# Token-major residual stream in a transformer kernel, with the first two weight blocks behind each norm taken per token tile

## The chip, the cores and the metric

The kernel runs on one NeuronCore of a Trainium2 chip, as one program with one launch. The metric is device time in microseconds of that core. TensorE (PE) multiplies, VectorE (DVE) and ScalarE (ACT) work elementwise, SyncE (SP) issues the weight DMAs, GpSimd (POOL) has next to nothing to do.

## The reference

256 tokens of width 1024 pass through six feed-forward blocks and four mixers (called ev, od, da and ga); a second sequence of 256 tokens, the context, passes through three of the feed-forwards and gives keys and values to the last two mixers. Each of the ten sublayers of x has a norm ahead and a norm on its output:

```python
def rms_norm(x, g, eps=1e-6):
    y = xf * lax.rsqrt(jnp.mean(xf * xf, axis=-1, keepdims=True) + eps)
    return (y * g.astype(jnp.float32)).astype(x.dtype)
...
def swiglu(h, w_gate, w_up, w_down):
    return (jax.nn.silu(h @ w_gate) * (h @ w_up)) @ w_down
```

A sublayer is h = h + rms_norm(f(rms_norm(h, g_pre) (+ shift)), g_post), with f a swiglu (1024 to 2816 to 1024) or a mixer that ends in a 1024x1024 output product. In the first four sublayers the gains are weights; in the last six of x and those of the context they and the shift come from a modulation product of a conditioning vector (the lane "a" below).

## The kernel before, in words

**Layout.** Both sequences lie with channels on partitions: H is [128, 8, 256], tile k holding channels 128k to 128k+127 of all 256 tokens. Every weight matrix is streamed from HBM in blocks of 1 MB (128x2048 fp32; `load_weights`, L202, into four RAW slots). Each block is split into two f32r halves: whi on ACT and wlo on DVE in two parts (`splits` and `other_half`, L210 and L235; three whi buffers, four wlo). An activation is kept as a high and a low f32r part as well, and a product is the sum of three: high*whi, low*whi, high*wlo (`three`, L267). A product on PE (L264) has a 128x128 piece of the weight block as its stationary operand and 256 tokens of one k as its moving one; a block of 8 k and two output tiles is 48 such products (`two_tiles`, L277).

**Down and output products.** A feed-forward of x has 22 blocks of gate and up and then, for each of four pairs of output tiles, three pieces of the down matrix over 22 k. Behind each output tile comes `put_out` (L345): ACT squares it, squares it times the gain, and copies it times the gain; DVE adds both squares to running sums and H*y to a third.

**Norm.** `norm` (L588) adds those sums over partitions on PE (L538), takes root and reciprocal (L525, L527), spreads them over the partitions by a product with ones (L553), and gets the sum of squares of the new residual out of the three sums. Then for k = 0 to 7 DVE scales y (L631), adds it to H (L637), weights it (L686), ACT makes the high part (L691, or L689 without a shift), DVE the low part (L700 or L698). `first_blocks` (L316) takes the two blocks behind the norm as the k come: two high products of each of two output tiles, then the low one, with the second block five k behind.

**Lanes.** One Python program writes the instructions of all engines, in one order. x is the main sequence; "c" (context) and "a" (modulation) are generators that are stepped in between. At a yield of kind "D" (before a block) and "d" (in the middle of one) `pace` (L1185) gives the others a turn; at a yield of kind "L" (a wait of so many us) `fill` (L1170) puts in context blocks and modulation blocks by a model clock. A norm of x has five such "L" yields. Attention waits for the context's keys with `want` (L1211).

The engines run their own instructions strictly in the order written, each waiting at semaphores.

## Time and profile before

| | |
|---|---|
| median of 3 runs | 2719.95 us (2719.37 to 2722.16) |
| the profiled execution, span | 2725.8 us |
| PE busy | 2528.6 us (93%), 20780 instructions |
| weight loads busy (overlap PE) | 2395.9 us (88%) |
| DVE busy | 1707.1 us (63%) |
| ACT busy | 1248.6 us (46%) |
| DMA | 480.14 MB, mean 176 GB/s |
| mean granted TensorE clock | 0.966 of full speed |

The page gives no time of the profiled execution beside its span; the span is what the prediction's sum is made against. Durations of single instructions overlap their neighbours': what an engine gives in a row is read from the starts, not from the durations.

### The profile page before, as it was taken

Reading aid. Unit: us, or ns where it says so; the run is one execution under the profiler, and the core shown is the slowest. Engines: PE = TensorE matmul, PEld = TensorE weight load, DVE = VectorE, ACT = ScalarE, POOL = GpSimd, SP = SyncE. Lnnn points to the kernel's source line nnn. Section 1 sums busy time; section 2 is a strip of 40 time slices with the busy share of each in tenths; the row PEclk is TensorE's granted clock in tenths of the full one; section 3 lists DMA queues with packets and bytes.
Section 4 is the critical chain, followed back from the end, with each engine's and each line's share of the span. In section 5 each row is a group of like instructions: output and inputs, shape, how many; then the busy total and the mean of one; then the engine's idle time right before and its main releaser. Section 6 shows DMA issues by size and latency. Waiting matters only on the chain.

```text
span 2725.8 us, 48854 instructions
## 1 busy us (share of the span) xinstructions
PE 2528.6 (93%) x20780; PEld 2395.9 (88%) x20780; DVE 1707.1 (63%) x2804; ACT 1248.6 (46%) x1697; POOL 1.2 (0%) x6
## 2 busy tenths in 40 slices
PE   6799997999999999999888998999999999887998
PEld 5689996888998999999887898999999999756997
DVE  6565574656766565566767576577655557646655
ACT  4443453444544444445445554455444345435443
POOL 0000000000000000000000000000000000000000
PEclk9899999999999999999898999999999999888999
DMA  6456656533555665544351344555545555363453
GB/s 218 181 200 242 241 203 229 189 109 124 186 202 216 236 226 196 211 147 154 132 174 52 120 171 154 185 175 173 179 170 179 180 177 183 114 215 137 170 178 116
DMA packets 71591, 480.14 MB, mean 176 GB/s; under 512 B 8784, under 2 KB 9296, under 8 KB 17744
## 3 DMA queue, kind: packets, MB, share of 16 engines
q1 hardware_dynamic: 66240, 468.74, 48.8%
q10 hardware_dynamic: 5136, 8.28, 1.0%
q8 instruction: 166, 2.72, 0.4%
q14 instruction: 49, 0.40, 0.0%
HBM read 471.48 MB, written 1.05 MB: 173 GB/s over the span
## 4 chain that ended last, share of the span: by engine, by line
PE 73%; DVE 13%; ACT 7%; DMA 4%; issue 3%; ACTq 0%; DVEq 0%
PE bank L264 64%; ACT whi L223 4%; DVE wlo L243 2%; DMA raw<-w_main 2%; DVE wlo L230 2%; PE bank L1115 2%; DMA raw<-w_down 1%; PE bank L997 1%; PE bank L935 1%; DVE ARX L686 1%; DVE HX L637 1%; DVE tmpx L631 1%; PE bank L985 1%; PE bank L553 0%; PE bank L1639 0%
## 5 line engine op out<-in xcount | busy, mean ns | idle before, releaser
L264 PE MATMUL bank<-HNX_hi,whi 128*128 128x256 f32 x2968 | 866.2, 293 | 64.3 <-DVE wlo L243 24.4
L223 ACT ACTIVATE whi<-raw 128x2048 fp32r<-128x2048 f32 (+1 forms) x378 | 705.5, 1868 | 334.6 <-PE bank L264 149.4
L264 PE MATMUL bank<-HNX_hi,wlo 128*128 128x256 f32 x2968 | 849.8, 287 | 0.0
L264 PE MATMUL bank<-HNX_lo,whi 128*128 128x256 f32 x2968 | 834.6, 286 | 0.0
L230 DVE TENSOR_TENSOR wlo<-raw,whi 128x1024 fp32r<-128x1024 f32 (+1 forms) x378 | 453.4, 1199 | 570.1 <-ACT whi L223 569.5
L264 PEld LDWEIGHTS bank<-HNX_hi,whi 128*128 128x128 f32 x2968 | 582.4, 196 | 91.7 <-issue 50.7
L264 PEld LDWEIGHTS bank<-HNX_hi,wlo 128*128 128x128 f32 x2968 | 583.1, 196 | 0.0
L264 PEld LDWEIGHTS bank<-HNX_lo,whi 128*128 128x128 f32 x2968 | 573.2, 196 | 1.1 <-issue 0.9
L243 DVE TENSOR_TENSOR wlo<-raw,whi 128x1024 fp32r<-128x1024 f32 (+1 forms) x378 | 450.8, 1193 | 0.0
L264 PE MATMUL bank<-HNC_hi,whi 128*128 128x256 f32 x1344 | 390.2, 290 | 11.6 <-DVE tmpc L448 4.5
L264 PE MATMUL bank<-HNC_lo,whi 128*128 128x256 f32 x1344 | 381.7, 284 | 0.0
L264 PE MATMUL bank<-HNC_hi,wlo 128*128 128x256 f32 x1344 | 381.6, 284 | 0.0
L264 PE MATMUL bank<-GX_hi,whi 128*128 128x256 f32 x1056 | 302.6, 287 | 4.0 <-DVE wlo L243 3.9
L264 PE MATMUL bank<-GX_lo,whi 128*128 128x256 f32 x1056 | 298.7, 283 | 0.0
L264 PE MATMUL bank<-GX_hi,wlo 128*128 128x256 f32 x1056 | 298.6, 283 | 0.0
L264 PEld LDWEIGHTS bank<-HNC_hi,whi 128*128 128x128 f32 x1344 | 259.2, 193 | 22.5 <-issue 7.9
L264 PEld LDWEIGHTS bank<-HNC_lo,whi 128*128 128x128 f32 x1344 | 259.4, 193 | 0.6 <-issue 0.2
L264 PEld LDWEIGHTS bank<-HNC_hi,wlo 128*128 128x128 f32 x1344 | 259.2, 193 | 0.0
L264 PEld LDWEIGHTS bank<-GX_hi,whi 128*128 128x128 f32 x1056 | 202.4, 192 | 10.4 <-DVE wlo L243 7.8
L264 PEld LDWEIGHTS bank<-GX_lo,whi 128*128 128x128 f32 x1056 | 202.5, 192 | 0.1
L264 PEld LDWEIGHTS bank<-GX_hi,wlo 128*128 128x128 f32 x1056 | 202.4, 192 | 0.0
L465 ACT ACTIVATE GX_hi<-tmpx 128x512 fp32r<-128x512 f32 x66 | 41.7, 632 | 250.0 <-DVE tmpx L461 250.0
(349 smaller groups left out, 2923.7 us busy)
## 6 DMA issues: line engine op xcount, KB each, us to landing
raw<-w_main SPq DMA_DIRECT2D x270, 1024.0 KB, 4.8
raw<-w_ada SPq DMA_DIRECT2D x72, 1024.0 KB, 4.8
raw<-w_down SPq DMA_DIRECT2D x72, 1024.0 KB, 4.9
raw<-w_down SPq DMA_DIRECT2D x36, 768.0 KB, 4.2
raw<-w_cmp SPq DMA_DIRECT2D x4, 1024.0 KB, 4.8
tmpx<-ARX ACTq DMA_DIRECT2D x18, 128.0 KB, 4.8
tmpx<-ARX ACTq DMA_DIRECT2D x32, 64.0 KB, 4.7
HX<-x_in SPq DMA_DIRECT2D x2, 512.0 KB, 6.0
```

The source lines that it names most:

```text
L223: NS.activation(WHI[q % HIS][:, 0:size], RAW[m % SLOTS][:, 0:size], ACT.Copy).then_inc(sems["w_hi"], 1)
L230: NV.tensor_tensor(WLO[m % SLOTS][:, 0:half], RAW[m % SLOTS][:, 0:half], WHI[q % HIS][:, 0:half].bitcast(fp32), SUB)
L243: NV.tensor_tensor(WLO[m % SLOTS][:, half:size], RAW[m % SLOTS][:, half:size], WHI[q % HIS][:, half:size].bitcast(fp32), SUB).then_inc(sem ...
L264: return NT.matmul(dst, (WHI[ordinal[n] % HIS], WLO[n % SLOTS])[w][:, k * 2 * P + col:k * 2 * P + col + P], x[xp][:, kx, :], start=start, ...
L465: NS.activation(g[0], S.TMP[p % 2][:, :], ACT.Copy).then_inc(hi.sem, 1)
L631: NV.tensor_tensor(S.TMP[k % 2][:, 0:T], S.Y[:, k, :], S.wide_y[:, 0:T], MUL).then_inc(sc.sem, 1)
L637: NV.tensor_tensor(S.H[:, k, :], S.H[:, k, :], S.TMP[k % 2][:, 0:T], ADD).then_inc(re.sem, 1)
L686: NV.scalar_tensor_tensor(S.Y[:, k, :], S.H[:, k, :], gain(k), S.wide_h[:, 0:T], MUL, MUL).then_inc(no.sem, 1)
L935: mm = NT.matmul(bank[:, c0 + c * T:c0 + (c + 1) * T], q[pr, :], k[pr, :], start=True, stop=True)
L985: mm = NT.transpose(turn_bank[:, c * P:(c + 1) * P], PB[w % 3][:, 0, c * P:(c + 1) * P], ident)
L997: mm = NT.matmul(out_bank[:, 0:P], v, PT[b][:, c * P:(c + 1) * P], start=c == 0, stop=c == len(vs) - 1)
L1115: mm = NT.matmul(bank[32 * g:32 * g + 32, 0:T], CCOL[:, k, 6 - 2 * r:38 - 2 * r], RAW[n % SLOTS][:, k * T:(k + 1) * T], start=r == 0 and k ...
```

## The change

The residual stream, and the context's, lie with tokens on partitions: H is [128, 2, 1024], token tile t holding tokens 128t to 128t+127. The hidden activations between a pre-norm and an output product keep channels on partitions.

- The down and output products have a tile of activations (128 k by 128 tokens) as stationary operand and 512 columns of the weights as moving one (`across`), for x; the context's have 256 columns. Their weights are laid out by rows on the host. `project` does them for x block by block, both token tiles of a block, but of the last three blocks (TAIL) first all of tile 0 and then all of tile 1.
- `put_out`, the column sums and the spreads go. The square sum of a token is an accumulated ACT square along the row (`square_of`); root and reciprocal are one column (`inverse`). `residual` weights by a gain laid out as a row (`row_of`: eight transposes of a column spread wide, and two copies), and adds to H.
- `scale_tile` scales the new residual, `turn_tile` transposes it (eight per token tile), `keep_tile` applies gain and shift and makes the high and low parts, per token tile.
- `first_blocks` takes both blocks for token tile 0, then both for tile 1, in products of 128 columns; `finish` brings tile 1's transposes and parts in between.
- The context's `norm` does the same with operations of 128x1024 (two squares, a weighting, an addition and a scaling per tile, and a root), then transposes and parts per tile. Its output product has its own copy of the weights (da_out_c).
- The input and the output are token-major, and the last store goes out per tile and half.

```diff
-SHORT_FIRST = ((0, 6), (6, 14), (14, 22))
+TAIL = 3
...
-            def first_blocks(S, n, dst, hi, lo):
...
+            def first_blocks(S, n, dst, early, finish=None):
+
+                for t in range(2):
+                    if t and finish is not None:
+                        early = finish()
+                    hi, lo = early[t]
+                    for b in range(2):
+                        if t == 0:
+                            landed(n + b)
+                        for j in range(KD + 2):
+                            for m in range(2):
+                                cols = slice(m * T + t * P, m * T + (t + 1) * P)
+                                if j < KD and on(pe, None if m or b else hi[j]):
+                                    for w in range(2):
+                                        by_tile(dst[b][:, cols], n + b, m * P, j, S.HN, t, 0, w, t == j == m == w == 0, False)
+                            for m in range(2):
+                                cols = slice(m * T + t * P, m * T + (t + 1) * P)
+                                if j >= 2 and on(pe, None if m or b else lo[j - 2]):
+                                    mm = by_tile(dst[b][:, cols], n + b, m * P, j - 2, S.HN, t, 1, 0, False, t == 1 and j == KD + 1)
+                        if t and pe:
                             mm.then_inc(sems["block_done"], 1)
-                splits(n + 1)
+                        if (t, b) != (0, 0):
+                            splits(n + b * t)
+
+            def by_tile(dst, n, col, k, x, t, xp, w, start, stop):
+
+                return NT.matmul(dst, (WHI[ordinal[n] % HIS], WLO[n % SLOTS])[w][:, k * 2 * P + col:k * 2 * P + col + P],
+                                 x[xp][:, k, t * P:(t + 1) * P], start=start, stop=stop, skip_group_check=True)
...
+            def across(dst, n, at, size, k, x, xp, t, w, start, stop):
+
+                return NT.matmul(dst, x[xp][:, k, t * P:(t + 1) * P], (WHI[ordinal[n] % HIS], WLO[n % SLOTS])[w][:, at:at + size], start=start, stop=stop)
...
+            def row_of(S, gain, known, bank):
+
+
+                t, marks = S.tag, known()
+                for h in range(2):
+                    put, row = up(f"{t}_row_in"), up(f"{t}_row")
+                    if on(pe, *marks, free.get(bank.name)):
+                        for k in range(4):
+                            mm = NT.transpose(bank[:, k * P:(k + 1) * P], gain(4 * h + k).to_broadcast([P, P]), ident)
+                        mm.then_inc(put.sem, 1)
+                    if on(act, put, free.get((t, "row"))):
+                        NS.activation(S.ROW[:, h * 2 * T:(h + 1) * 2 * T], bank[:, :], ACT.Copy).then_inc(row.sem, 1)
+                    free[bank.name] = row
...
+            def residual(S, t, srcs):
+
+                sq, wt, re = [], [], []
+                for h, (bank, mark) in enumerate(srcs):
+                    sq.append(square_of(S, bank[:, :], SQ2[:, :], 8 * t + h, mark, now(f"{S.tag}_square")))
+                    if h:
+                        rs, root, inv = inverse(S, t, 0, sq)
+                    wt.append(up(f"{S.tag}_weighted"))
+                    if on(dve, sq[h], None if h or t else now(f"{S.tag}_row")):
+                        NV.tensor_tensor(half(S.Y, t, h), bank[:, :], S.ROW[:, h * 2 * T:(h + 1) * 2 * T], MUL).then_inc(wt[h].sem, 1)
+                    free[bank.name] = wt[h]
+                free[S.tag, "row"] = wt[1]
+                if on(dve, root):
+                    NV.reciprocal(rs, rs).then_inc(inv.sem, 1)
+                for h in range(2):
+                    re.append(up(f"{S.tag}_resid"))
+                    if on(dve, wt[h], inv):
+                        NV.scalar_tensor_tensor(half(S.H, t, h), half(S.Y, t, h), rs, half(S.H, t, h), MUL, ADD).then_inc(re[h].sem, 1)
+                return re
...
+            def scale_tile(S, t, ready):
+
+                sq = []
+                for h in range(2):
+                    sq.append(square_of(S, half(S.H, t, h), half(S.Y, t, h), 8 * t + 4 + h, ready[h]))
+                rs, root, inv = inverse(S, t, 4, sq)
+                if on(dve, root):
+                    NV.reciprocal(rs, rs).then_inc(inv.sem, 1)
+                sc = [up(f"{S.tag}_scaled"), up(f"{S.tag}_scaled_high")]
+                if on(dve, inv):
+                    NV.tensor_scalar(half(S.Y, t, 0), half(S.H, t, 0), rs, None, MUL).then_inc(sc[0].sem, 1)
+                if on(act, inv, ready[1]):
+                    NS.activation(half(S.Y, t, 1), half(S.H, t, 1), ACT.Copy, scale=rs).then_inc(sc[1].sem, 1)
+                return sc
...
+            def turn_tile(S, t, scaled):
+
+                turned = []
+                for b, bank in enumerate(S.turn[t]):
+                    turned.append(up(f"{S.tag}_turned"))
+                    if on(pe, scaled[b], free.get(bank.name)):
+                        for k in range(4):
+                            mm = NT.transpose(bank[:, k * P:(k + 1) * P], S.Y[:, t, (4 * b + k) * P:(4 * b + k + 1) * P], ident)
+                        mm.then_inc(turned[b].sem, 1)
+                return turned
...
+            def keep_tile(S, t, turned, pre, mods):
+
+                gain, shift = pre
+                his, los, cols = [], [], slice(t * P, (t + 1) * P)
...
+                        NV.tensor_tensor(S.HN[1][:, k:k + 2, cols], full, S.HN[0][:, k:k + 2, cols].bitcast(fp32), SUB).then_inc(lo.sem, 1)
+                    los.extend((lo, lo))
+                for b, bank in enumerate(S.turn[t]):
+                    parts = [(k, bank[:, k % 4 * P:(k % 4 + 1) * P]) for k in range(4 * b, 4 * b + 4)]
+                    for k, src in parts:
...
+                        if on(act, turned[b]):
+                            if shift is None:
+                                NS.activation(S.HN[0][:, k, cols], src, ACT.Copy, scale=gain(k)).then_inc(his[k].sem, 1)
+                            else:
+                                NS.activation(S.HN[0][:, k, cols], src, ACT.Identity, bias=shift(k), scale=gain(k)).then_inc(his[k].sem, 1)
+                    for k, src in parts:
+                        if shift is None:
...
+                            if on(dve, his[-1]):
+                                NV.scalar_tensor_tensor(S.HN[1][:, k, cols], src, gain(k), S.HN[0][:, k, cols].bitcast(fp32), MUL, SUB).then_inc(los[k].sem, 1)
+                            free[bank.name] = los[k]
+                            continue
+                        free[bank.name] = up(f"{S.tag}_normed")
+                        if on(dve, his[-1]):
+                            NV.tensor_scalar(S.TMP[k // 4][:, k % 4 * P:(k % 4 + 1) * P], src, gain(k), shift(k), MUL, ADD).then_inc(free[bank.name].sem, 1)
+                        if k % 2:
+                            low(k - 1)
+                return his, los
...
+            def project(S, blocks, x, waits, row, pre, mods=lambda: (), then=None):
...
+                def part(n, b, t):
+                    for h in range(2):
+                        bank, last = acc[t][h], b == nb - 1
+                        if b == 0:
+                            on(pe, free.get(bank.name))
+                        for j in range(2):
+                            if on(pe, *waits.get(2 * b + j, ()) if t == h == 0 else ()):
+                                for w, xp in ((0, 0), (0, 1), (1, 0)):
+                                    mm = across(bank[:, :], n, j * D + h * 2 * T, 2 * T, 2 * b + j, x, xp, t, w,
+                                                b == j == 0 and (w, xp) == (0, 0), last and j == 1 and w == 1)
...
+                    if t == 1 and pe:
+                        mm.then_inc(sems["block_done"], 1)
...
+                for b in range(nb - TAIL):
+                    yield ("D",)
+                    n = take(S.tag, *blocks[b])
+                    landed(n)
+                    part(n, b, 0)
+                    splits(n, apart=True)
...
+                    part(n, b, 1)
+                    other_half()
+                    if b == 0 and row:
+                        row_of(S, *row, BANK[4])
+                known = mods()
...
+                ns = [take(S.tag, *blocks[b]) for b in range(nb - TAIL, nb)]
...
+                table_of(ACT.Sqrt)
+                for j, n in enumerate(ns):
+                    landed(n)
+                    part(n, nb - TAIL + j, 0)
+                    if j == 0:
+                        splits(n)
...
+                first = residual(S, 0, [(acc[0][h], marks[0, h]) for h in range(2)])
+                if pre:
+                    first_scaled = scale_tile(S, 0, first)
+                for j, n in enumerate(ns):
+                    if j == TAIL - 1 and pre:
+                        turned = turn_tile(S, 0, first_scaled)
+                        kept = [[keep_tile(S, 0, turned, pre, known)]]
+                    part(n, nb - TAIL + j, 1)
+                    if j < TAIL - 1:
+                        splits(n + 1)
+                        yield ("d",)
...
+                second = residual(S, 1, [(acc[1][h], marks[1, h]) for h in range(2)])
...
+                    return first + second
+                second_scaled = scale_tile(S, 1, second)
                 if then is not None:
                     table_of(then)
...
+                kept[1:] = [lambda: [None, keep_tile(S, 1, turn_tile(S, 1, second_scaled), pre, ())]]
+                return kept
...
+            def opening(S, pre, loads):
+
+                scaled = [scale_tile(S, t, [loads[t]] * 2) for t in range(2)]
+                splits(-1, most=1)
+                kept = [[keep_tile(S, 0, turn_tile(S, 0, scaled[0]), pre, ())]]
+                splits(-1)
+                return [*kept, lambda: [None, keep_tile(S, 1, turn_tile(S, 1, scaled[1]), pre, ())]]
```

## Rows read from the trace of the kernel before

**Rows 1.** The page, section 1: busy time, share of the span, instructions.

```profile
PE 2528.6 (93%) x20780; PEld 2395.9 (88%) x20780; DVE 1707.1 (63%) x2804; ACT 1248.6 (46%) x1697; POOL 1.2 (0%) x6
```

**Rows 2.** Timeline of PE in ffn 5: start us, us, engine, line, operation, tiles.

```profile
2600.20 0.28 PE L264 MATMUL bank<-HNX_lo,whi 128*128 128x256 f32 x1
2600.32 0.28 PE L264 MATMUL bank<-HNX_hi,wlo 128*128 128x256 f32 x1
```

**Rows 3.** The same where the clock stood at half.

```profile
1312.26 0.41 PE L264 MATMUL bank<-HNX_hi,whi 128*128 128x256 f32 x1
1312.47 0.41 PE L264 MATMUL bank<-HNX_hi,wlo 128*128 128x256 f32 x1
```

**Rows 4.** Timeline of PEld: loads of eight products of one column, and the next.

```profile
665.63 0.97 PEld L793 LDWEIGHTS bank<-VEC,tmpx 128*128 128x128 f32 x8 [1.02 <-ACT tmpx L786]
666.51 0.19 PEld L264 LDWEIGHTS bank<-GC_hi,whi 128*128 128x128 f32 x1
```

**Rows 5.** Lines L264 and L793: duration ns min/median/max, first and last start, forms.

```profile
L264 PEld LDWEIGHTS bank<-HNX_hi,whi x2968: 186/192/333, 19.2 to 2647.5; 128*128 128x128 f32 x198
...
L793 PEld LDWEIGHTS bank<-VEC,tmpx x24: 186/192/192, 665.6 to 1554.3; 128*128 128x128 f32 x24
```

**Rows 6.** Stretches around nine X norms: us, busy of each engine, clock, DMA, GB/s.

```profile
core 0: us, PE busy (x) PEld busy (x) DVE busy (x) ACT busy (x) POOL busy (x), PEclk, DMA share, GB/s
356.00:403.60 47.60, 44.40 (x365) 43.05 (x363) 36.53 (x69) 24.96 (x31) 0.00 (x0) 0.96 0.49 170
...
2504.50:2531.20 26.70, 18.50 (x127) 15.58 (x126) 23.85 (x57) 13.60 (x22) 0.00 (x0) 0.74 0.21 73
sum 343.00, PE 289.71 PEld 271.08 DVE 273.24 ACT 173.91 POOL 0.00; mean PE 32.19 PEld 30.12 DVE 30.36 ACT 19.32 POOL 0.00
```

**Rows 7.** The same, tile HNC_hi alone: PE, PEld, DVE, ACT.

```profile
356.00:403.60 47.60, 31.95 (x160) 26.41 (x159) 0.00 (x0) 0.00 (x0) 0.96 0.49 170
...
1622.40:1662.20 39.80, 18.11 (x96) 14.97 (x95) 0.00 (x0) 0.00 (x0) 0.91 0.37 128
```

**Rows 8.** Stretches of ffn 0 and ffn 5, columns as in the first stretches.

```profile
200.00:350.00 150.00, 148.27 (x1308) 139.25 (x1307) 77.92 (x96) 57.73 (x58) 0.00 (x0) 1.00 0.68 246
...
2525.00:2700.00 175.00, 173.54 (x1446) 173.33 (x1445) 103.21 (x119) 76.51 (x72) 0.00 (x0) 1.00 0.51 175
```

**Rows 9.** Groups of instructions: busy us, mean ns of one, idle before.

```profile
L223 ACT ACTIVATE whi<-raw 128x2048 fp32r<-128x2048 f32 (+1 forms) x378 | 705.5, 1868 | 334.6 <-PE bank L264 149.4
L230 DVE TENSOR_TENSOR wlo<-raw,whi 128x1024 fp32r<-128x1024 f32 (+1 forms) x378 | 453.4, 1199 | 570.1 <-ACT whi L223 569.5
...
L461 DVE SCALAR_TENSOR_TENSOR tmpx<-tmpx,bank 128x512 f32<-128x512 f32 x66 | 45.3, 686 | 63.9 <-PE bank L264 63.3
...
L973 ACT ACTIVATE ARX<-bank,SMALL 128x512 f32<-128x512 f32 x48 | 32.4, 681 | 9.8 <-DVE SMALL L964 9.8
L533 ACT ACT_TABLE_LOAD x19 | 24.4, 1283 | 0.7 <-ACT ARX L356 0.4
L973 ACT ACTIVATION_READ_ACCUMULATOR ARX<-bank,SMALL 128x1 f32 x48 | 9.6, 200 | 0.0
L719 ACT ACTIVATE HNX_hi<-bank 128x128 fp32r<-128x128 f32 x8 | 2.2, 278 | 5.6 <-PE bank L1639 5.6
L721 DVE TENSOR_TENSOR HNX_lo<-bank,HNX_hi 128x128 fp32r<-128x128 f32 x8 | 2.3, 292 | 14.6 <-ACT HNX_hi L719 14.6
```

**Rows 10.** Timeline of DVE in the last norm: two operations in a row.

```profile
2717.89 0.42 DVE L631 TENSOR_TENSOR tmpx<-ARX,bank 128x256 f32<-128x256 f32 x1
2718.23 0.42 DVE L637 TENSOR_TENSOR HX<-HX,tmpx 128x256 f32<-128x256 f32 x1
```

**Rows 11.** Timeline of PE: four transposes and what follows.

```profile
1479.95 0.60 PE L985 MATMUL bank<-VEC,ARX 128*128 128x128 f32 x4
1480.39 0.61 PE L997 MATMUL bank<-ARX 128*128 128x128 f32 x4
```

**Rows 12.** Timeline of the kernel's end: the last product and the stores.

```profile
2711.20 0.28 PE L264 MATMUL bank<-GX_hi,wlo 128*128 128x256 f32 x1
...
2718.68 4.62 SPq L1915 DMA_DIRECT2D out<-HX  x4
```

561 lines of the change are left out of this document (193 added, 368 removed).

## The prediction

> **What bounds the kernel now.** I read the page first, then the products themselves, then the stretches around the norms, then what ACT and DVE take for the operations that the change adds. The reader is to see four things.
>
> PE is busy 93% of the span [rows 1], so PE's own work counts almost everywhere. In the long dense stretches one f32r product of 256 columns starts every 0.12 us [rows 2]. At half clock the spacing is 0.21 us [rows 3]: 256 columns at 1.2 GHz, so streaming a column costs 0.83 ns there and 0.42 ns at full clock (107 ns for 256, 53 ns for 128).
>
> A product also has a weight load. Eight products of one single column, with 128x128 loads, have their loads in 0.97 us [rows 4]; less the 0.19 us that one load lasts, 0.78 us for seven steps, 0.111 us each. There is nothing to stream in them, so 0.111 us is the rate of loading 128x128. Those operands are fp32 and ours f32r, but an f32r load lasts the same at least, 186 ns against 186 ns [rows 5]. So a 256-column product (107 ns of stream, 111 ns of load) has its two halves just balanced. A narrower product is held up by its load, a wider one hides it.
>
> The third thing is the X norms. Nine stretches run from X's last product ahead of a norm to the end of the first two blocks behind it: 343.0 us in all [rows 6]. In five of them context blocks fill the wait: 48 products a block, five blocks in four stretches and three in one. The HNC_hi records (two of three products) are 160 and 96 [rows 7], so 240 and 144 products; 4*240+144 = 1104 products * 0.12 = 132 us. What the norms themselves take is 211 us, 23.4 us each, of which 96 products * 0.12 = 11.5 us are the two blocks.
>
> The fourth is that ffn 0 (and ffn 1) are held by DMA: 246 GB/s with 0.68 of the queues busy, against 175 GB/s and 0.51 in ffn 5 [rows 8].
>
> **The change, part by part.**
>
> *Wide products.* X's down and output products go from 256 to 512 columns: 528 to 264 in each of six ffns, 192 to 96 in each of four outputs, so 1968 pairs become 1968 singles. A pair costs 0.24 us now. A wide one streams 2*107 = 213 ns, with a load that fits under it. Bounds: 0.213 (gain 27 ns each, 53 us) and 0.24 (gain nothing). I take 0.216, gain 24 ns, as half-clock products already go at their stream's rate: 47 us. In ffn 0 and ffn 1 the weights come no sooner, so 2*264*24 ns = 13 us of it are lost. **-34 us.**
>
> *First two blocks per token tile.* Each norm's 96 products of 256 become 192 of 128, each with its own load. Bounds: 0.053 us by stream, 0.12 us if the present spacing is a load's. I take 0.112, the one-column rate. PE then needs 21.5 us for the two blocks instead of 11.5, 100 us over ten norms. Part of that lies where PE waits today, so the norm has to be walked through.
>
> *The norm itself.* Removed: put_out (three ACT and four DVE operations per 128x256 tile), the column sums, two spreads through PE, and per k the scale, add, weight and low part that now hand hi tiles to PE. Put in their place, counted from T0, the end of tile 0's last product. Tile 1's products of the last three blocks (36 * 0.216 = 7.8 us) cover tile 0's chain.
> - Durations [rows 9]: ACT 128x512 about 0.68 us plus 0.20 for the accumulator, DVE 128x512 0.69, ACT 128x128 0.28, DVE 128x128 0.29, split 1.87 on ACT and two halves of 1.20 on DVE. Queued neighbours start earlier than they end: 0.42 us operations 0.34 us apart [rows 10], so about 0.08 comes off each.
> - Tile 0: squares to 1.1, root 1.5, reciprocal 1.9, two residual halves 3.4, squares 4.3, root 4.6, reciprocal 4.8, scaled 5.4. PE reaches the transposes at 5.2 and waits 0.3. Four transposes take 0.44 us [rows 11], eight 0.9. PE ends tile 1's last part at 9.0.
> - ACT and DVE are queues in order. The splits of the next two blocks stand ahead of keep_tile(0), because the three tail blocks hold all three whi buffers until tile 1 is through: ACT 5.4 to 9.2, DVE 7.4 to 12.0. Then ACT makes eight highs (to 10.9) and DVE eight normed parts and four lows (to 15.0). PE starts the first block at 9.7, and is stopped at the third k until the first low at 12.8. First block done 17.3, second 22.7.
> - Tile 1: its squares stand behind keep_tile(0) on ACT, its weighting behind the same on DVE, so although PE is done at 9.0 the chain starts at 15.0; scaled at 19.9, table load 1.28, split of the third block. That is hidden by PE's 22.7. Transposes to 23.6, first high 24.1, first low 26.2 (a wait of 1.2), blocks done 36.1.
> So from the end of tile 1's products: 27.1 us, and 1.2 us ahead of it, 28.3 us; in the three of nine norms without a shift DVE has 8 operations instead of 12, twice, and I take 27.2. 6*28.3+3*27.2 = 251 against 211. **+41 us.** Bounds: 23.3 us (192*0.112 + 1.8 of transposes, every chain hidden) gives 0; 33 us (each wait double, 0.12 a product) gives +86.
>
> *Opening.* Squares of a tile need only its own half of x, but the weight splits and 21.5 us of products follow: first product near 17.5 instead of 19.2, end near 40 instead of 37. **+3.**
>
> *row_of.* Gains are laid out as a row by eight transposes, in two rounds on one bank: PE's second four wait for ACT's copy of the first. It stands 14 times (ten for X, four for the context), 8*0.11 = 0.9 us each, and a wait that is at least the copy's 0.6 us and up to 2.5 behind a split on ACT; nothing is between on PE, so it hides nothing. I take 0.9. **+25** (bounds +17 and +48).
>
> *Context lane.* Five norms get 80 transposes (+9) and lose their sums and spreads (-6). Its products in the new layout are as many and as wide: 0. Its long 128x1024 operations sit in front of X's splits; PE has two blocks of lead there, 0 to +5. The norms filled 23 context blocks so far, and project gives fewer turns to the lane; these blocks run later, at the same price, but their waits may come into the open ahead of the attentions. **+13** (bounds 0 and +50).
>
> *Prefetch.* The first two blocks keep their raw slots until tile 1 is through, so two of four slots stay full some 20 us. Where DMA is the bound, about 2 us come back at each of four norms. **+8** (0 to +20).
>
> *End.* Last product to the end is 14.2 us now: a root, a spread, sixteen DVE operations of 0.34 us in a row, and the stores [rows 12]. With tile 0 long done, it is one chain of about 3.5 us and a store. **-7.**
>
> *The Trainium skill on this.* The 0.111 us of the one-column products is what "TensorE: Matmul & The Clock Gate", section "LDWEIGHTS (loading the stationary operand)", gives: columns over 1.2 GHz, 107 ns for 128, whatever is streamed. The same page, "Back-to-back issue gap", names about 81 ns for a stream of load and 128-column product pairs. That speaks for the change's narrow products; the one-column row speaks against it. With 81 ns the ten norms would take 1920*31 ns = 60 us less of PE; it is weighed as a rival below.
>
> **Sum.** -34 +41 +3 +25 +13 +8 -7 = +49, on the profiled 2725.8 us: 2775. The median of the runs lies 5.9 below that span, so **2769 us**.
>
> **Rivals.**
> 1. *Narrow products cheap*: what a 256-column product takes beyond its stream (0.12 less 0.107) is all that a load adds, so one of 128 takes 53+13 = 66 ns, and the chain of tile 1 lies under them. At 66 ns the two blocks take 12.7 us; with transposes 1.8 and 1 us of wait a norm takes 15.5, 9*(15.5-23.4) = -71. With -34, +3, +18, +3, -7: -88, a median of 2632. For it: nothing in this trace shows a 128-column f32r product. Against: [rows 4]. And the walk-through shows that even at 66 ns DVE's order (split, split, keep, residual, split, keep) puts the end at about 33 instead of 36.1, so products alone give 3 us a norm, about 2740. The sign turns where a norm falls below 23 us. The 81 ns of the skill's page would be this rival's dearer half.
> 2. *Chains hidden, loads not.* If ACT and DVE get through in the shadow of 21.5 us, a norm takes 23.3 to 24.5 and the sum is +5: medians 2710 to 2730. For it: DVE is busy 273 of these 343 us today [rows 6], mostly with work that goes. Against: the order of the queues.
> 3. *Context lane late.* 23 blocks are pushed behind, and attention waits for its keys with X idle: the forecast plus 40, 2810. For it: nine filled or unfilled norms have no filler in the new code. Against: the lane ran one block to one through ffn 2 to ffn 4, and it has slack before both attentions.
>
> **Chances.** Forecast 0.58 (its own range 2735 to 2805), rival 1 0.11, rival 2 0.17, rival 3 0.14. The measurement tells about 0.2% from no change, some 5 us. Faster by more: rival 1 and half of rival 2 and a little of the forecast, 0.21. Within: 0.08. Slower: 0.71. The range 2700 to 2825 leaves out rival 1's lower half and the tail of rival 3.
>
> **What would show it.** Right: starts of 128-column f32r products 0.11 us apart; 512-column ones 0.216; a norm (last product to the end of the two blocks) of 27 to 29 us with PE waiting at the third k on HNX_lo; PE waits at row_of on ACT. Wrong: 128-column products 0.06 to 0.09 apart; norms under 23 us; context blocks alone, without X, ahead of an attention.

## The result, and the profile after

The changed kernel takes **3010.45 us** (median of four runs, 2992.35 to 3037.28) where the kernel before takes 2720.14: 1.104 times as long, 95% interval 1.100 to 1.108. The forecast was 2769 with a range of 2700 to 2825. The sign was right; the loss was forecast at 49 us and is 290. The profiled execution has a span of 3001.6 us, 275.8 more than before. One of its four runs, 3037.28, counts as a slow one and is left out of the ratio; the other three lie 25 us apart.

The page first (sections 1 and 2, against [rows 1]):

```profile
PE 2759.0 (92%) x19714; PEld 2548.6 (85%) x19714; DVE 1548.3 (52%) x2331; ACT 1272.1 (42%) x1752; POOL 1.2 (0%) x6
...
PEclk9989989999899978999897979999899997979799
```

PE has 1066 instructions fewer and is busy 230 us longer. PE's idle time grew by 45 us only (197.2 to 242.6), so it is not waits that were added in the first place: products last longer. The granted clock shows it, 0.924 of full speed as a mean against 0.966.

The timeline of PE, in the form of [rows 2] and [rows 3] (start us, us, engine, line, operation, tiles). First two of the wide products, then narrow ones in the norm ahead of ffn 0, then in the norm behind the diff attention (ahead of ffn 3):

```profile
344.74 0.39 PE L263 MATMUL bank<-whi,GX_hi 128*128 128x512 f32 x1
344.97 0.40 PE L263 MATMUL bank<-whi,GX_lo 128*128 128x512 f32 x1
...
170.39 0.28 PE L341 MATMUL bank<-HNX_hi,whi 128*128 128x128 f32 x1
170.50 0.28 PE L341 MATMUL bank<-HNX_hi,wlo 128*128 128x128 f32 x1
...
1769.62 0.45 PE L341 MATMUL bank<-HNX_hi,whi 128*128 128x128 f32 x1 [6.64 <-DVE tmpx L589]
1769.87 0.42 PE L341 MATMUL bank<-HNX_hi,wlo 128*128 128x128 f32 x1
1770.08 0.41 PE L341 MATMUL bank<-HNX_hi,whi 128*128 128x128 f32 x1
```

A narrow product takes 0.11 us at full clock, as forecast, but **0.21 us at half clock**. And most of them ran at half clock. The stretches from X's last wide product to the end of the two blocks, as [rows 6] (us, busy time of each engine, granted clock, DMA share, GB/s), here without filler in them:

```profile
141.00:179.50 38.50, 33.74 (x202) 33.76 (x203) 13.41 (x31) 12.28 (x32) 0.00 (x0) 0.69 0.17 59
...
1763.00:1812.50 49.50, 42.88 (x201) 42.81 (x202) 20.06 (x41) 15.53 (x33) 0.00 (x0) 0.54 0.13 46
...
sum 383.60, PE 331.82 PEld 330.68 DVE 156.91 ACT 123.07 POOL 0.00; mean PE 36.87 PEld 36.74 DVE 17.43 ACT 13.67 POOL 0.00
```

383.6 us for nine norms, against 211 before and 251 in the forecast: 172.6 of the 275.8 us. In such a norm the clock's half-speed stretch begins in the wait ahead of the first product, or at its end. In six norms it ends just behind the beginning of tile 1 (23.9 us long in five, 27.3 in one), in three it goes through both tiles (48 to 51 us). One norm of each kind, cut between the tiles:

```profile
145.80:167.90 22.10, 22.10 (x105) 22.09 (x105) 5.76 (x11) 6.49 (x12) 0.00 (x0) 0.50 0.00 1
167.90:179.50 11.60, 11.60 (x100) 11.60 (x99) 2.85 (x9) 2.26 (x8) 0.00 (x0) 0.94 0.27 92
1769.60:1791.80 22.20, 22.18 (x105) 22.10 (x105) 6.29 (x12) 6.54 (x12) 0.00 (x0) 0.50 0.00 1
1791.80:1812.50 20.70, 20.70 (x99) 20.70 (x98) 7.30 (x15) 4.75 (x9) 0.00 (x0) 0.50 0.16 51
```

PE is busy without a gap, and still at 0.50 for 22 us through tile 0 (so in all nine norms) and for 43 us in the second. In the first, the clock rises at 169.4, 1.5 us behind tile 1's first product. The first cause to test was therefore: does the wait bring the clock down, or do the narrow products, or does it need both? A second suspect was the context lane: of the other 103 us, 23.2 are the opening, and the two stretches between norms that hold the diff and the global attention are some 51 us longer, if each product of the context in them is taken out at 0.12 us (an estimate from the spacing in [rows 2]).

### The profile page after: what moved, and what is told of

Its sections match the earlier page's. It is cut to its first block, busy times and chain, and to the rows that moved or that the text cites. A ratio compares the mean times of both kernels' runs of the same rounds, so it can differ in the third digit from the quotient of the medians.

```text
span 3001.6 us, 45997 instructions
## 1 busy us (share of the span) xinstructions
PE 2759.0 (92%) x19714; PEld 2548.6 (85%) x19714; DVE 1548.3 (52%) x2331; ACT 1272.1 (42%) x1752; POOL 1.2 (0%) x6
## 4 chain that ended last, share of the span: by engine, by line
PE 79%; DVE 9%; ACT 6%; DMA 3%; issue 3%; ACTq 0%; DVEq 0%
PE bank L258 40%; PE bank L263 18%; PE bank L341 12%; ACT whi L217 3%; DMA raw<-w_main 2%; DVE wlo L237 2%; PE bank L1124 1%; DVE wlo L224 1%; PE bank L1000 1%; DVE tmpc L589 1%; PE bank L554 1%; PE bank L938 1%; DMA raw<-w_down_x 1%; PE bank L988 1%; ACT ARC L681 0%
## 5 line engine op out<-in xcount | busy, mean ns | idle before, releaser
L258 PE MATMUL bank<-HNX_hi,whi 128*128 128x256 f32 x2392 | 690.2, 289 | 37.7 <-DVE wlo L237 26.1
L258 PE MATMUL bank<-HNX_lo,whi 128*128 128x256 f32 x2392 | 682.3, 285 | 0.0
L258 PE MATMUL bank<-HNX_hi,wlo 128*128 128x256 f32 x2392 | 681.9, 285 | 0.0
L258 PEld LDWEIGHTS bank<-HNX_hi,whi 128*128 128x128 f32 x2392 | 464.6, 194 | 51.3 <-issue 35.7
L258 PEld LDWEIGHTS bank<-HNX_lo,whi 128*128 128x128 f32 x2392 | 464.8, 194 | 0.5 <-issue 0.5
L341 PE MATMUL bank<-HNX_hi,whi 128*128 128x128 f32 x640 | 237.4, 379 | 58.8 <-DVE tmpx L589 32.3
L341 PEld LDWEIGHTS bank<-HNX_hi,whi 128*128 128x128 f32 x640 | 188.5, 295 | 63.3 <-issue 55.3
L341 PE MATMUL bank<-HNX_hi,wlo 128*128 128x128 f32 x640 | 236.0, 377 | 0.0
L263 PE MATMUL bank<-whi,GX_hi 128*128 128x512 f32 x528 | 211.9, 401 | 8.0 <-DVE wlo L237 7.9
L263 PE MATMUL bank<-whi,GX_lo 128*128 128x512 f32 x528 | 207.7, 393 | 0.0
L263 PE MATMUL bank<-wlo,GX_hi 128*128 128x512 f32 x528 | 207.6, 393 | 0.0
```

The source lines that it names most:

```text
L258: return NT.matmul(dst, (WHI[ordinal[n] % HIS], WLO[n % SLOTS])[w][:, k * 2 * P + col:k * 2 * P + col + P], x[xp][:, kx, :], start=start, ...
L263: return NT.matmul(dst, x[xp][:, k, t * P:(t + 1) * P], (WHI[ordinal[n] % HIS], WLO[n % SLOTS])[w][:, at:at + size], start=start, stop=stop)
L341: return NT.matmul(dst, (WHI[ordinal[n] % HIS], WLO[n % SLOTS])[w][:, k * 2 * P + col:k * 2 * P + col + P], x[xp][:, k, t * P:(t + 1) * P] ...
```

## The experiments

All kernels were timed beside the kernel before; times are medians, ratios are to the kernel before, with 95% intervals. What a kernel saves against the changed one is the difference of the medians, from 3010.45; by the ratios it is up to 8 us less, and it is uncertain by 11 to 17 us.

**Four edits to tell the clock, the load and the lane apart.**

The first two blocks once, with 256 columns, behind both tiles:

```
-                for t in range(2):
-                    if t and finish is not None:
-                        early = finish()
+                (hi0, lo0), (hi1, lo1) = early[0], finish()[1]
...
-                                        by_tile(dst[b][:, cols], n + b, m * P, j, S.HN, t, 0, w, t == j == m == w == 0, False)
+                                    product(dst[b][:, m * T:(m + 1) * T], n + b, m * P, j, S.HN, 0, j, w, j == m == w == 0, False, True)
```

> The changed kernel, but its first two blocks wait for both token tiles and run once, in products of 256 columns, as before the change; the rest of the change stays. Theory A (the products of 128 columns themselves let the granted clock fall to half and hold it there): the second tile's chain is no longer covered, so the PE waits some 14.5 us between the last product of a projection and the first product, then 96 products take 11.5 us at 0.12 us each: about 27 us for each of the nine norms, where the changed kernel takes 42.6 on average, 15 x 9 = 135 us less, and up to 50 us less again where the half clock outlives the two blocks. 2820 to 2880 us; half clock in all under 250 us of the span, where the changed kernel has 459. Rival B (the wait ahead of the first product lets the clock fall, whatever the products are): the wait is longer here, the 256-column products run 0.21 us apart, a norm takes 14.5 + 20 = 35 us or more, and the time is 2920 us or more with the half clock at 350 us or more. Rival C (the late context lane carries the loss): 2960 us or more, since the lane is as late as in the changed kernel.

Measured: **2823.72 us** (1.037, 1.035 to 1.040), 187 us less than the changed kernel. The chain of tile 1 is bare now, so PE waits longer, and yet nine norms take 235.8 us instead of 383.6. The norm behind the diff attention, cut at its first product and at the clock's rise:

```profile
1657.60:1672.00 14.40, 1.94 (x9) 1.60 (x9) 10.40 (x24) 9.38 (x24) 0.00 (x0) 0.64 0.22 84
1672.00:1675.20 3.20, 3.20 (x15) 3.20 (x16) 2.20 (x7) 3.20 (x8) 0.00 (x0) 0.51 0.00 0
1675.20:1685.20 10.00, 10.00 (x85) 10.00 (x85) 7.39 (x13) 3.30 (x3) 0.00 (x0) 1.00 0.32 107
```

The wait does bring the clock down, as rival B had it, but with 256 columns it is back 3.2 us after the first product (1.5 to 5.1 us in the nine norms). Rival B's consequence (20 us of products at half clock) didn't come. Theory A had under 250 us at half clock; it is 274.

The kernel before, each 256-column product of the two blocks as two of 128:

```
-                                product(dst[0][:, m * T:(m + 1) * T], n, m * P, j, S.HN, 0, j, w, j == 0 and m == 0 and w == 0, False, True)
+                                two_products(dst[0][:, m * T:(m + 1) * T], n, m * P, j, S.HN, 0, j, w, j == 0 and m == 0 and w == 0, False, True)
...
+                for t in range(2):
+                    cols = slice(t * P, (t + 1) * P)
+                    mm = NT.matmul(dst[:, cols], (WHI[ordinal[n] % HIS], WLO[n % SLOTS])[w][:, k * 2 * P + col:k * 2 * P + col + P],
+                                   x[xp][:, kx, cols], start=start and t == 0, stop=stop, skip_group_check=True)
```

> The kernel before with one edit: each product of 256 columns in the first two blocks becomes two products of 128 columns, one for each token tile, with the same weights loaded twice; order, chains and context work stay as they were. 96 products become 192 at ten places. Theory A (these products let the clock fall): 192 x 0.213 = 40.9 us in place of 11.5 us at most of the ten places, so +200 to +290 us, 2920 to 3010 us, with the half clock over 350 us of the span where the kernel before has under 200. Rival B (the clock falls for the wait ahead of them; as a price the load alone, 0.112 us): 192 x 0.112 = 21.5 us in place of 11.5, +100 us at most, 2760 to 2820 us, half clock as before. Rival C (the context lane) says the same as B here.

Measured: **2925.98 us** (1.076, 1.074 to 1.077), +204 us for this edit alone. It split by place. Four of the ten:

```profile
798.00:819.60 21.60, 21.60 (x196) 21.60 (x195) 12.63 (x26) 6.71 (x9) 0.00 (x0) 1.00 0.28 99
1089.90:1111.40 21.50, 21.50 (x195) 21.50 (x194) 12.29 (x24) 7.12 (x9) 0.00 (x0) 1.00 0.28 99
1378.70:1419.90 41.20, 41.20 (x195) 41.20 (x195) 13.54 (x28) 8.28 (x11) 0.00 (x0) 0.50 0.08 26
1744.40:1785.60 41.20, 41.18 (x193) 41.20 (x194) 14.24 (x29) 7.75 (x10) 0.00 (x0) 0.50 0.07 26
```

Where context blocks had kept PE busy up to the first product (three places) all 192 went at 0.112 us. Where the clock was already at half they went at 0.213 to the end. At one place (2093.2) it fell 2.2 us behind a wait of 1.59 us and stayed down. So the narrow products don't bring the clock down by themselves, and in none of these places did they bring it back. In the changed kernel they didn't in any tile 0; but in six of its nine norms the clock came back 1.3 to 1.8 us behind the first product of tile 1, with nothing on PE but transposes and narrow products. What brought it back there, no run shows.

The changed kernel, every narrow product streaming its 128 columns twice, into both halves of the bank (so the two token tiles get mixed in it):

```
-                                cols = slice(m * T + t * P, m * T + (t + 1) * P)
+                                cols = slice(m * T, (m + 1) * T)
...
-                                 x[xp][:, k, t * P:(t + 1) * P], start=start, stop=stop, skip_group_check=True)
+                                 x[xp][:, k, t * P:(t + 1) * P].unsqueeze(1).to_broadcast([P, 2, P]), start=start, stop=stop, skip_group_check=True)
```

> The changed kernel, with each product of 128 columns in the first two blocks reading its 128 columns twice, so that it streams 256 columns into both halves of the bank; the output is not the reference's. The loads, waits and order of the changed kernel stay, only the stream doubles. Theory A (the 128-column stream behind a load lets the clock fall): at full clock a product now takes 0.12 us, 192 x 0.12 = 23 us in a norm, so norms of about 29 us in place of 42.6 and 2830 to 2900 us in all, although the columns double; half clock under 250 us. Rival B (the waits let the clock fall): the products are 0.21 us apart as in the changed kernel, 3000 to 3030 us, half clock still over 400 us. Load-bound rival (0.112 us whatever the clock): 192 x 0.008 x 10 = 15 us more, 3025 us.

Measured: **2889.22 us** (1.062, 1.060 to 1.063), 121 us less, though TensorE streams twice the columns in them. The same wait as at 1769.62 above, and what follows:

```profile
1707.05 0.55 PE L341 MATMUL bank<-HNX_hi,whi 128*128 128x256 f32 x1 [6.67 <-DVE tmpx L589]
```

```profile
1707.00:1711.20 4.20, 4.15 (x19) 4.18 (x20) 3.30 (x8) 1.78 (x6) 0.00 (x0) 0.50 0.00 0
1711.20:1720.00 8.80, 8.80 (x76) 8.80 (x75) 3.01 (x4) 4.21 (x5) 0.00 (x0) 1.00 0.01 2
```

4 us at half clock in place of 43; in all nine norms the clock is back 2.8 to 5.0 us behind the first product. Nine norms take 292.3 us, the opening's blocks 26.3 instead of 42.8.

The changed kernel with context or modulation work ahead of the two blocks:

```
                 if then is not None:
                     table_of(then)
+                yield ("L", 6.5)
```

> The changed kernel with 14 us of context or modulation work put between a projection's last product and the first two blocks, where the kernel before had some; nothing else moves. Theory A: the waits ahead of the first products (5 to 7 us in five norms) are covered, and the context lane is in time again at the diff attention and the global attention (idle and half-speed stretches of some 26 and 30 us there), so 50 to 80 us less, 2930 to 2960 us, while the narrow products still run 0.213 us apart and the half clock stays over 350 us. Rival B (the wait lets the clock fall): with no wait ahead of them the narrow products run at 0.112 us, 10 us less in each of nine norms beside the same 50 to 80: 2840 to 2880 us, half clock under 250 us. Rival C (the context lane carries the larger part): under 2900 us with the half clock in the norms unchanged.

Measured: **2933.78 us** (1.076, 1.073 to 1.080), 77 us less. The time at half clock (from the records of the granted clock) went down by 101 us, to 358: both mechanisms are in it. For the lane, the products of HNC_hi from the end of ffn 4 to the end of X's wait ahead of ffn 5 (the first product of its two blocks), in before, after and this kernel:

```profile
2314.40:2516.10 201.70, 13.94 (x64) 11.80 (x64) 3.82 (x8) 4.07 (x8) 0.87 0.46 160
```

```profile
2507.00:2780.90 273.90, 33.85 (x160) 28.63 (x160) 3.40 (x8) 5.92 (x16) 0.82 0.40 137
```

```profile
2488.80:2714.60 225.80, 13.41 (x64) 11.32 (x64) 3.40 (x8) 5.79 (x16) 0.82 0.44 148
```

The changed kernel has 96 more of them there (two of three products of a block), at a place where X has nothing to do, and PE waits 12.3 us at once for the context's norm:

```profile
PE bank L554 <- DVE ARC L704: 12.3, 1, 12.3
```

With the work back ahead of the norms this stretch is 48 us shorter. That is rival 3's mechanism, shown ahead of the global attention. Of the 72 us that the stretch has grown since before, 23 are the norm in it (49.7 instead of 26.9 us).

**The wait covered by work that does nothing.**

```
+                    on(pe, free.get(S.pair[0].name))
+                    keep_busy(S.pair[0])
...
+                    for _ in range(48):
+                        NT.matmul(bank[:, 0:T], some[:, 0:P], some[:, 0:T], start=True, stop=True)
```

> The changed kernel with one thing added: ahead of each first product of the first two blocks, TensorE runs 48 extra bf16 products of 256 columns on constants, into the first block's own bank, which the first real product overwrites. They take about 5.2 us, in the time in which it waited for the second block's bank (idle 4.8 to 6.9 us in the nine norms). Nothing is removed and all later products of 128 columns stay. Theory D (what the four kernels so far show taken together: the wait lets the granted clock fall, and the products of 128 columns then don't bring it back, where 256-column ones do within 3 to 14 us): without the wait the clock stays, the narrow products run 0.112 us apart, each norm is 11 to 20 us shorter, 110 to 160 us less in all: 2850 to 2900 us, half clock under 300 us of the span. Rival E (the narrow stream lets the clock fall by itself): 3010 to 3030 us, the half clock as in the changed kernel.

Measured: **2888.48 us** (1.063, 1.059 to 1.066), 122 us less by adding 480 products. Four of its nine norms, and the sum:

```profile
120.70:148.50 27.80, 27.78 (x249) 26.95 (x248) 13.43 (x31) 12.39 (x32) 0.00 (x0) 1.00 0.23 85
...
1033.30:1063.80 30.50, 28.23 (x249) 26.99 (x248) 20.05 (x41) 15.63 (x33) 0.00 (x0) 1.00 0.22 77
...
1678.40:1708.90 30.50, 28.21 (x249) 26.97 (x248) 20.08 (x41) 15.63 (x33) 0.00 (x0) 1.00 0.21 75
...
2403.10:2440.30 37.20, 34.84 (x249) 33.43 (x246) 19.75 (x40) 13.85 (x31) 0.00 (x0) 0.81 0.18 64
...
sum 283.80, PE 272.90 PEld 263.07 DVE 156.11 ACT 121.75 POOL 0.00; mean PE 30.32 PEld 29.23 DVE 17.35 ACT 13.53 POOL 0.00
```

Norms 100 us shorter, the opening's blocks 20 us (22.8 instead of 42.8): that is the whole gain. The three norms without a shift have no wait at all and take 27.8 us. The six with a shift wait once more, at tile 1's first low part (and four of them still 1.45 to 1.54 us ahead of the first product); the waits of three of them:

```profile
1054.21 0.44 PE L349 MATMUL bank<-HNX_lo,whi 128*128 128x128 f32 x2 [0.71 <-DVE HNX_lo L580]
...
1699.31 0.44 PE L349 MATMUL bank<-HNX_lo,whi 128*128 128x128 f32 x2 [0.72 <-DVE HNX_lo L580]
...
2424.18 0.44 PE L349 MATMUL bank<-HNX_lo,whi 128*128 128x128 f32 x2 [0.71 <-DVE HNX_lo L580]
```

Behind the first two the clock stayed; behind the third it fell 2.2 us later and the rest of the blocks ran at half. Of the six, three fell and three didn't, with waits of 0.71 or 0.72 us all. Over this kernel, the one with filler and the one with both cures (below), the same wait within narrow products at full clock stands thirteen times, and seven times the clock fell 0.4 to 2.7 us behind it. Ten times all 192 narrow products began at full clock and had no wait among them (three in the kernel before with narrow products, two with filler, three here, two with both cures), and it never fell. In the trace of before, one wait of that size ahead of 256-column products, with no fall behind it:

```profile
684.60 0.36 PE L264 MATMUL bank<-HNX_hi,whi 128*128 128x256 f32 x1 [0.76 <-DVE HNX_lo L721]
```

```profile
683.50:697.50 14.00, 13.24 (x117) 12.34 (x117) 9.78 (x16) 7.10 (x12) 0.00 (x0) 1.00 0.61 221
```
So within narrow products a wait of 0.7 us was followed by the fall in about half of the cases, and what decides it isn't shown. The 25 us between the changed kernel's three runs, with mean clocks of 0.916 to 0.924, fit that; it was not tried apart.

**Both cures at once, with the narrow products kept.**

```
+                sparing[0] = BANK[3]
+                yield ("L", 6.5)
+                sparing[0] = None
...
+                if spare[0] is not None and start + us - clock[0] > 0.5:
+                    keep_busy(spare[0], round((start + us - clock[0]) / 0.107))
```

> The changed kernel, its products of 128 columns kept, with both cures at once: 14 us of context or modulation work ahead of the first blocks, as in the kernel with filler (2934 us), and extra bf16 products on constants, as in the kernel kept busy (2888 us), only at the opening (60) and where no such work is at hand (50, 61, 7 and 50 in four norms). It asks whether the rest of the prediction's sum holds once the clock and the context lane are as it assumed. Against the kernel with filler: the opening 17 us shorter, and the norms of 39.1, 48.2, 49.7 and 41.9 us with the narrow products at half clock 11 to 20 us shorter where the clock now holds, 45 to 70 us in all: 2850 to 2875 us. If the two costs are the whole miss, under 2800 us. If the clock still falls in most of these norms, over 2890 us.

Measured: **2884.44 us** (1.060, 1.057 to 1.063), 49 us less than with filler alone and 9 to 34 above what was expected. In five norms the clock fell within the two blocks, each time in or behind a wait (0.71, 0.72, 1.72, 3.64 and 5.52 us). The two longest are in the norms ahead of ffn 0 and of ffn 5, where PE now came to the second block before its low weights were there; the second one, and the first with what follows it:

```profile
2688.05 0.47 PE L343 MATMUL bank<-HNX_hi,whi 128*128 128x128 f32 x1 [5.52 <-DVE wlo L239]
```

```profile
137.14 0.33 PE L343 MATMUL bank<-HNX_hi,whi 128*128 128x128 f32 x1 [3.64 <-DVE wlo L239]
```

```profile
137.30:169.60 32.30, 32.30 (x153) 32.29 (x154) 4.91 (x11) 2.78 (x9) 0.00 (x0) 0.50 0.10 33
```

The cures don't add up: 2884 is no less than the 2888 of the kernel kept busy alone (their intervals overlap), and it is 115 us above the forecast.

**The other terms.** Row made once for each lane, at its first use; the twelve other makings are left out, and later norms use that first row:

```
                 t, marks = S.tag, known()
+                if (t, "row") in free:
+                    return
```

> The changed kernel with the row of gains made only once for each lane, at its first use, and that row used for every later norm, so the output is not the reference's; this leaves out 12 of the 14 makings, each of eight transposes with two waits of TensorE for ScalarE's copy. The prediction priced one at 1.8 us (0.9 of transposes, 0.9 of waits), bounds 17 to 48 us for all: so 2985 to 2995 us, 22 us less. If the waits, some of which fall at half clock, also let the clock fall, more than 40 us less. If nothing of it lies on the path, no change.

Measured: **2969.18 us** (1.092, 1.087 to 1.097): 0.012 of the time, 34 us by the ratios, with some 17 us either way (its profiled execution has 20 us more at half clock, 479 instead of 459). The price was 22 for these twelve; the waits of PE in the changed kernel are 13.8 us (rowx, ten) and 7.9 us (rowc, four), the transposes 12.6.

256-column first blocks and filler together, then the same with each wide product as two of 256; the edit that makes the second out of the first:

> Two edits together: the first two blocks in products of 256 columns once both tiles are there (2824 us alone), and some 14 us of context or modulation work between a projection's last product and them. The chain that was left bare, 8 us of idle in the last 10 ahead of the first product and about 12 in 20, is covered in the norms where work is at hand, which is work that is needed elsewhere anyhow: 9 x 11 = 100 us less at most, and the clock no longer falls there. 2700 to 2760 us. If the context lane has no work ready in half of the norms, 2760 to 2790 us.

> The kernel with 256-column first blocks and filler, with each of the 1968 products of 512 columns in X's projections split into two of 256 columns, the same stationary operand loaded twice. The trace of the changed kernel has the wide product at 0.227 us and a 256-column one at 0.120 us: 1968 x 0.013 = 26 us more than the kernel with filler. By the price of the prediction, 0.216 us for a wide product, it would be 1968 x 0.024 = 47 us more.

```
-                                    mm = across(bank[:, :], n, j * D + h * 2 * T, 2 * T, 2 * b + j, x, xp, t, w,
+                                    for c in range(2):
+                                        mm = across(bank[:, c * T:(c + 1) * T], n, j * D + (2 * h + c) * T, T, 2 * b + j, x, xp, t, w,
```

Measured: **2770.79 us** (1.019, 1.018 to 1.021), and **2786.08 us** (1.025, 1.023 to 1.026). The first is the changed kernel without narrow products and with the lane's work back ahead of the norms: what is left of the change (the token layout, wide products, rows, the shorter end, and tile 1's chain, now bare, for which PE waits 45.8 us in five norms) is 52 us slower than before. The second says what the wide products are worth, 15 us with some 6 either way, not 34.

**Three tries for a better kernel.** First, the kernel with 256-column first blocks and filler, its filler raised from 6.5 to 10 in the plan, with extra products where the plan finds no other work; second, the same with rows in two banks; third, the extra products alone in the kernel before the change:

```
+                for h, bank in enumerate(banks):
+                    puts.append(up(f"{t}_row_in"))
...
-                            row_of(S, *gain, BANK[0])
+                            row_of(S, *gain, (BANK[0], BANK[1]))
```

> The kernel with 256-column first blocks and filler, its filler target raised from 6.5 to 10 in the program's plan, and where the plan finds no context or modulation work to put in (four of the nine norms), 82 or 93 extra bf16 products of 256 columns on constants in the time in which the chain is bare (idle of 11 to 14 us there). They add no work to the path if they end before the chain does (8.8 and 10 us), and by theory D (a wait lets the clock fall) they keep the granted clock: 4 norms x 6 us of first blocks and chain transposes at half clock, 15 to 25 us less than 2771: 2745 to 2760 us, half clock 60 us shorter. If the clock fell for another reason, 2770 to 2775 us.

> The kernel before this one in the list, with the row of gains made in two banks: its eight transposes run back to back and ScalarE copies the two halves behind them, so TensorE no longer waits for the first copy. The trace has those waits at 12.3 us for lane x (ten, longest 1.6) and under 8 us for lane c: 10 to 20 us less than the kernel before it in the list. If the time that leaving out 12 rows saved (41 us) was the copies' place on ScalarE and not TensorE's wait, no change.

> The kernel before the change with extra bf16 products of 256 columns on constants in the waits of X's norm, only where the program's plan has no context or modulation work for them: 9 to 33 at a time, about 84 in each of four norms, and 28 at the opening. The rows of before have the granted clock at half around the first blocks of five places (124.6 to 145.1, 1302.2 to 1315.9, 1643.6 to 1650.4, 2319.4 to 2333.1, 2507.1 to 2520.8), each behind idle of 2 to 7 us. Theory D: the clock stays up in four of them, 3 to 5 us less in each, 2703 to 2712 us. Where the planned place of the extra products isn't the place of the wait, they stand in the way: up to 9 us of TensorE in each of four norms, 2720 to 2755 us.

Measured: **2786.11 us** (1.024, 1.023 to 1.026), 15 us more, not less; **2771.61 us** (1.019, 1.018 to 1.021), 15 less than that; **2735.15 us** (1.006, 1.004 to 1.007), 15 more than before. The first and the third held the clock (half-clock time 226 to 196 us, and 188 to 156) and lost all the same. Where it could be looked at, the extra products stood in the way. At the first norm of the first kernel the chain's transposes stand at 122.49 without extra products; with them, the extra products start 2.9 us late, since their bank is released late, and the transposes come only at 126.57:

```profile
122.49 1.94 PE L548 MATMUL bank<-VEC,ARX 128*128 128x128 f32 x8 [8.91 <-DVE ARX L536]
```

```profile
115.92 10.81 PE L345 MATMUL bank<-VEC 128*128 128x256 bf16 x82 [2.91 <-DVE HNX_lo L587]
126.57 0.60 PE L557 MATMUL bank<-VEC,ARX 128*128 128x128 f32 x4
```

The first has a second loss, from its other plan: ahead of ffn 4, PE waits 9.4 us at the first product, where it waited 0.2 us without.

No kernel of the study beats the kernel before.

## Why the prediction was right or wrong

**Wide products, -34.** The term was mis-sized at "I take 0.216". They stand 0.227 us apart (median of 1808; 0.224 to 0.24), 13 ns less than a pair, not 24; 1968 times 13 ns is 26 us, and splitting them again cost 15. A product of 256 or of 512 columns takes 13 to 14 ns more than its stream (107 and 213), so a longer stream, under which the load would fit, doesn't hide that gap; at half clock, 0.213 for 256 columns, it isn't seen. Each of these products has its own load, so the runs can't tell a cost of the load from one of the product.

**Narrow products at full clock, 0.112.** Right, 0.11 apart, and rival 1 is out. The Trainium skill's page "TensorE: Matmul & The Clock Gate" has about 81 ns for such pairs ("Back-to-back issue gap"). In its section "LDWEIGHTS (loading the stationary operand)" a load takes its columns over 1.2 GHz, by estimate 107 ns for 128. The narrow products of the changed kernel stand 0.108 to 0.116 us apart at full clock, so for these f32r operands the second is the nearer one; at half clock, 0.213, neither holds.

**The norms, +41.** This is the step that failed and decided the case: each narrow product was priced at full clock, "192*0.112". The trace of before held the warning: in [rows 6] the stretch at 2504.5 has a clock of 0.74, and [rows 3] are first blocks behind a norm's wait. The prediction used [rows 3] for the streaming rate only, and never asked at which clock the new products would run, nor what a load takes at half clock. It takes 0.213 us, twice as long. The trace of before had that too, in eight one-column products at half clock, against [rows 4]:

```profile
1307.38 1.78 PEld L793 LDWEIGHTS bank<-VEC,tmpc 128*128 128x128 f32 x8 [0.90 <-ACT tmpc L786]
```

With one column there is nothing to stream, and they start 0.213 us apart instead of 0.111. So it is the load that doubles, and the narrow product is held up by it at either level.

The walk-through itself held in the main: at full clock (wait covered) a norm takes 27.8 us without a shift and 28.8 to 30.5 with one, against 27.2 and 28.3. ACT and DVE went through in the order given, tile 1's chain was hidden, and the wait at tile 1's first low part is there, 0.71 us instead of 1.2. One wait was misplaced. PE was to start at hi 0 and stop at the third k. But the code waits for both banks of X.pair before the first block, BANK[4] also holds half of tile 0's transposes, and DVE's last read of it is the last part of keep_tile(0), so PE stood 6.64 us ahead of the first product. That wait costs little by itself, as the kernel kept busy shows (0.5 to 2.2 us above the price with the wait filled but not shortened), but the clock goes down in it. Sum: +172.6, of which the clock is about 100 (the changed kernel against the one kept busy) and some 22 more where it fell in three norms even there. The 51 that are left stand against the 41 of the forecast.

**Opening, +3.** +23.2: the first product came at 17.5 as forecast, the 192 products took 42.8 us at 0.213, and 22.8 when extra products stood ahead of them. The same step failed.

**row_of, +25.** 34 with 17 either way for twelve of fourteen: inside the bounds of 17 to 48, above the value taken.

**Context lane, +13, and prefetch, +8.** Too small. What is left over once norms, opening and end are taken out is 89 us (275.8 - 172.6 - 23.2 + 8.7); with -15 to -26 for the wide products and 34 for the rows, some 70 to 80 us remain for the two terms of 21. The eight stretches between the nine norms, as sums, before and after:

```profile
sum 2070.90, PE 1976.70 PEld 1870.69 DVE 1254.37 ACT 944.61 POOL 0.00; mean PE 247.09 PEld 233.84 DVE 156.80 ACT 118.08 POOL 0.00
```

```profile
sum 2290.30, PE 2138.52 PEld 1952.20 DVE 1235.85 ACT 1017.27 POOL 0.00; mean PE 267.31 PEld 244.03 DVE 154.48 ACT 127.16 POOL 0.00
```

They are 219 us longer, 132 of them context products that stood in the norms before. PE's idle time in them went from 94.2 to 151.8 us, +58. By what ended the waits, over the whole trace: 21.7 us for the copies of the rows; 12.3 for the context's norm; 11.5 more for low weight halves (28.6 to 40.1), which is where a late prefetch would show; 10.2 more within the attentions (21.7 to 31.9), most of it in the diff attention, whose stretch has some 720 context products instead of 1010 to put in between. PE's busy time at half clock went from 72 to 110 us there, worth at most 19. Filler ahead of the two blocks brought 68 us of span back, part of it clock. The argument against rival 3, "it has slack before both attentions", was not read from a row and was wrong ahead of the global attention. No run takes the lane, the prefetch and the clock outside the norms apart, so how the rest divides stays open.

**End, -7.** Right, nearly: from the last product to the end 14.2 us before, 5.5 after, -8.7.

**The rivals.** Rival 1 fell. Rival 2's chains were indeed hidden, at a price nobody had put on the products; its sum of +5 doesn't follow from its own norms of 23.3 to 24.5 us, which give +7 to +18, and nothing hangs on that here. Rival 3 came true in addition to the forecast, not instead of it; adding its 40 to the forecast would still have stayed 200 us short. No rival had the clock in it, so the range, built from costs of loads and waits, couldn't reach the result. That the sign was right doesn't hang on the clock: by estimate it cost some 142 us (100 and 22 in the norms, 20 at the opening), and without it the loss would still be near 150 us, three times the forecast.

## What to carry to other kernels

Before pricing a matmul, ask which clock it will have where it stands, and look at the granted clock of the same place in the trace before. Splitting products into narrow ones to start earlier cost twice here, at the load (0.112 us where half of a 256-column product is 0.06) and at the clock, and it was worst just behind a wait, where one wants it. If a wait can't be avoided ahead of narrow products, put useful wide ones into it, and check that a plan's idea of where the wait is agrees with the trace.

## What the runs showed of the hardware

- At half clock a 128-column f32r product with its own load takes 0.213 us, a 256-column one 0.213 and a one-column fp32 one 0.213: the load slows down with the array, from 0.111 to 0.213 us.
- TensorE, busy without a gap with narrow products, stayed at 1.2 GHz for 22 us in all nine norms and for 43 us in three, while products that stream 256 columns, behind the same 6.7 us wait, had 2.4 GHz after 4 us. The Trainium skill (page "TensorE: Matmul & The Clock Gate", "Part 1: The HAM clock gate (the "warmup" mystery)") tells of a clock set by how busy the engine has been recently. Here PE's busy share was 1.00 in both stretches, and the granted clock 0.50 in one and 1.00 in the other. In six norms the clock came back among narrow products after all, 1.3 to 1.8 us into tile 1, for a reason that no run shows.
- Narrow products kept 2.4 GHz where it was there and nothing interrupted them (192 in 21.5 to 24 us, ten places of ten); a wait of 0.7 us among them was followed by the fall in seven cases of thirteen.
- At the opening the granted clock reads 1.00 while the products stand 0.21 us apart. The same stretch in the changed kernel and in the one kept busy:

```profile
17.50:60.30 42.80, 42.80 (x201) 42.80 (x202) 6.71 (x12) 5.41 (x12) 0.63 (x1) 1.00 0.18 67
```

```profile
17.10:39.90 22.80, 22.78 (x202) 22.54 (x203) 6.71 (x12) 5.40 (x12) 0.63 (x1) 1.00 0.33 124
```

  Some 200 products in 42.8 us and in 22.8 us, under one and the same figure: that early in these executions the spacing tells the clock, the figure in the clock's column doesn't.
